# Dilated attention in a four-layer trunk: TensorE's weighted sums move between the two shares of the projection

## The chip, the cores and the metric

The kernel runs on one core of one Trainium2 chip. The metric is the device time of one execution in microseconds. Before the change it is 2908.95 us, the median of three runs (2908.55 to 2910.62).

## The reference

One sequence of 512 tokens, width 1024, four layers. Every layer is a token mixer and a squared-ReLU MLP, each behind an RMS norm and added to the residual. The mixers by layer are: dilated attention, indexer-selected sparse attention, gated DeltaNet, dilated attention. Only the two dilated ones (layers 0 and 3) are touched.

```python
qkv = (h @ w_in).reshape(B, S, 3, A_N_GROUPS, A_HEADS, HEAD_DIM)
q = rms_norm(qkv[:, :, 0], q_gain)          # per head
k = rms_norm(qkv[:, :, 1], k_gain)
for g, (window, dilation) in enumerate(((128, 1), (512, 4), (2048, 16))):
    o, lse = dilated_window_attention(q[:, :, g], k[:, :, g], v[:, :, g], bias_g, window, dilation)
wts = softmax(stack(lses), axis=0)          # mixture of the three dilations
y = sum(wts[..., None] * stack(outs), axis=0)
return y.reshape(B, S, A_OUT) @ w_out
```

## The kernel before

All matrix products with weights run as three products of rounded parts (high x high, high x low, low x high). ACT rounds a weight chunk to its high part (`rounding`, L695), GpSimd subtracts to get the low part (`split`, L555), TensorE multiplies. Every engine has its own list of instructions in program order, and semaphores tie the lists together; the order is written out by hand.

A dilated mixer works on heads in pairs: 4 pairs of 8 units, 32 units in all. Units 0 to 3 of a pair are the near group's four token blocks (one or two key blocks each), units 4 to 7 the two far groups, by residue class. A unit goes through this pipeline, and step s of a loop over 36 steps holds one stage of several units:

- TensorE `scores(s)` (L1856, L1863): queries times keys into banks 2 and 3. It waits until both halves of the logits of unit s-1 are out of these banks (`al_done`).
- DVE `logits(s)` (L1225): adds the bias and keeps the row's extreme value.
- ACT `probs(s)` (L868): exponential with a row sum, two halves.
- DVE `inverses(s-1)` (L1234): reciprocal of the sums, one step later.
- GpSimd `weights_scaled(s-1)` (L578): scales the probabilities by them.
- TensorE `turn(s-2)` (L1877): transposes them into bank 4 or 5.
- DVE (L1308), for the last pair ACT (L907): copies the transposes to SBUF.
- TensorE `weigh(s-3)` (L1893): weighted sum of the values, into bank 6. It waits for that copy.
- DVE `outputs(s-3)` (L1244): takes the sum out of bank 6.

Between these, TensorE computes the query and key projections of the next pairs: 18 tiles of 24 large matmuls (L1674), cut by `a_share` into 52 shares, two per step: `fill(2s)` and `fill(2s+1)`. So the shares end with step 25. A finished tile goes ACT square (L800) and copy with gain (L801), on DVE an epsilon term (L1208), then `sum_qk` on TensorE (L1801), which is issued at the end of the share after the one in which the tile ended; then ACT logarithm and exponential (L818, L820) and GpSimd `qk_scale` (L567). A tile's second half of a chunk also starts `rounding` and `split` of the chunk after next.

From step 26 on `joined` (L1719) puts parts of the output projection into the steps. At step 8f+1 `difference` (L1907) spreads the log sums of a finished pair, which DVE clamps (L1257), ACT turns into mixing weights at step 8f+2 (L897, L899, L901), and DVE mixes at step 8f+3 (L1263, L1266, L1268). ACT rounds the result (L911) and DVE takes its low part (L1272).

In a step, ACT's order is: `probs(s)`, the mixing operations if any, `part(2s)` (mean squares of a tile ended in share 2s-1, then square and copy of a tile ended in share 2s), the copy of unit s-2 for the last pair, `part(2s+1)`. DVE's order is: `inverses(s-1)`, `outputs(s-3)`, `logits(s)`, log sums, `part(2s)` (epsilon terms), mixing, the copy of unit s-2, `part(2s+1)`. GpSimd's is: `weights_scaled(s-1)`, second half of a split, the query or key scalings, first half of a split.

TensorE's two rules around the shares are:

```python
# fill(G): matmuls lo..hi of the tiles, then
for k, n, t in a_ended(i, G - 1):
    sum_qk(0, a_q(i, k, n, t))
# a_share(G): total = 24 * 6 * 3 = 432, A_FILL = 52
return min(total, total * G // A_FILL), min(total, total * (G + 1) // A_FILL)
```

Of the kernel before, what the change touches and what calls it, by code (L numbers as in the profile page):

```python
# [45 lines left out]
A_UNITS = A_PAIR_UNITS * A_PAIRS  # L46
# [51 lines left out]
def trunk(nc, x_in, rel_bias, params, c_gates, masks, bucket_rows, bias_mask, mlp_w1, mlp_w2,  # L98
# [20 lines left out]
    with ExitStack() as ctx:  # L119
# [287 lines left out]
        def a_blocks(u):  # L407

            return 1 if u % A_PAIR_UNITS == 0 else 2

        def a_near(u):
            return u % A_PAIR_UNITS < NB
# [6 lines left out]
        def a_share(G):  # L419

            total = 24 * 6 * (A_PAIRS - 1)
            return min(total, total * G // A_FILL), min(total, total * (G + 1) // A_FILL)

        def a_tiles(i):

            return [(k, chunk_at["aqk", i, k], tile0[chunk_at["aqk", i, k]] + j)
                    for k in range(3, 3 * A_PAIRS) for j in range(2)]

        def a_ended(i, G):

            lo, hi = a_share(G)
            return [x for j, x in enumerate(a_tiles(i)) if lo < 24 * j + 24 <= hi] if G >= 0 else []

        def a_q(i, k, n, t):

            return q_first[i] + 2 * k + t - tile0[n]
# [1202 lines left out]
        def _(pe):  # L1639
# [63 lines left out]
            def joined(i, j, pairs, lo, hi):  # L1703

                n0 = chunk_at["ao", i, 0]
                last = pairs[-1] == A_PAIRS - 1
                t = tile0[n0 + last] + j
                if lo == 0:
                    pe.wait_ge(w_lo_done, n0 + 1)
                    pe.wait_ge(*evac[t - 2])  # L1710
                for k in range(lo, hi):
                    f, z = pairs[k // 3], k % 3
                    if f >= 2 and z == 0:
                        pe.wait_ge(w_lo_done, n0 + 2)
                    w, a = ((w_hi, g_hi), (w_hi, g_lo), (w_lo, g_hi))[z]
                    c = DM * (f % 2) + P * j
                    if z == 0:
                        pe.wait_ge(yl_done, y_first[i] + f + 1)
                    mm = nc.tensor.matmul(lin_bank[t % 2][:], w[(n0 + f // 2) % 2][:].rearrange("p k n -> p (k n)")[:, c:c + P],  # L1719
                                          a[:, f, :], start=k == 0, stop=k == 3 * len(pairs) - 1)  # L1720
                if hi == 3 * len(pairs):
                    mm.then_inc(lin_done, 1)
# [69 lines left out]
            def sum_qk(kind, Q):  # L1792

                pe.wait_ge(qsq_done, Q + 1)
                if Q:
                    pe.wait_ge(qln_done, Q)
                if spread[0]:
                    pe.wait_ge(aclamp_done, spread[0])
                summed[0] = Q + 1
                sqs = mem[kind]["sq"]  # L1800
                nc.tensor.matmul(stat_bank[:], halves, sqs[Q % len(sqs)], start=True, stop=True).then_inc(ssq_done, 1)  # L1801

            def mixer_a(li, i):
                U0, F0, Q, Y = first_a[i], first_pair[i], q_first[i], y_first[i]

                def tile(n, t, lo, hi, act_sem=None):
                    product(n, t, H, CT, lo, hi, act_sem, 16 * li, None)
# [23 lines left out]
                def fill(G):  # L1831

                    lo, hi = a_share(G)
                    for j, (k, n, t) in enumerate(a_tiles(i)):
                        a, b = max(lo, 24 * j), min(hi, 24 * j + 24)
                        if a < b:
                            tile(n, t, a - 24 * j, b - 24 * j)
                    for k, n, t in a_ended(i, G - 1):
                        sum_qk(0, a_q(i, k, n, t))

                def scores(u):

                    f, z = divmod(u, A_PAIR_UNITS)
                    if z == 0:
                        pe.wait_ge(qk_ready, Q + 6 * f + 2)
                    if z == NB:
                        pe.wait_ge(qk_ready, Q + 6 * f + 6)
                    if u == 0:
                        pe.wait_ge(copied, copy_first[i] + 12)
                    if U0 + u:  # L1850
                        pe.wait_ge(al_done, 2 * (U0 + u))
                    if a_near(u):
                        n, k0 = P * a_blocks(u), P * max(z - 1, 0)
                        for half in range(2):
                            r = slice(HD * half, HD * half + HD)
                            mm = nc.tensor.matmul(bank[2 + half][:, 0:n], aq[f % 2][0][r, P * z:P * z + P],  # L1856
                                                  aq[f % 2][1][r, k0:k0 + n], start=True, stop=True)
                    else:
                        cols = slice(P * (z - NB), P * (z - NB) + P)
                        for g in (1, 2):  # L1860
                            for half in range(2):
                                r = slice(HD * half, HD * half + HD)
                                mm = nc.tensor.matmul(bank[2 + half][:, P * (g - 1):P * g],  # L1863
                                                      aq[f % 2][2 * g][r, cols], aq[f % 2][2 * g + 1][r, cols],
                                                      start=True, stop=True)
                    mm.then_inc(as_done, 1)

                def turn(u):

                    pe.wait_ge(an_done, 2 * (U0 + u + 1))  # L1870
                    if U0 + u >= 2:
                        pe.wait_ge(at_copied, U0 + u - 1)
                    nb = a_blocks(u)
                    for half in range(2):
                        for k in range(nb):
                            c = P * (nb * half + k)
                            mm = nc.tensor.transpose(bank[4 + u % 2][:, c:c + P], al[u % 4][:, half, P * k:P * k + P],  # L1877
                                                     ident)
                    mm.then_inc(at_turned, 1)

                def weigh(u):

                    f, z = divmod(u, A_PAIR_UNITS)
                    nb = a_blocks(u)
                    pe.wait_ge(at_copied, U0 + u + 1)
                    if U0 + u:
                        pe.wait_ge(ao_done, U0 + u)
                    for k in range(nb):
                        b, g = (z + 1 - nb + k, 0) if a_near(u) else (z - NB, 1 + k)
                        for half in range(2):  # L1890
                            c = (g * A_HEADS + 2 * f + half) * HD
                            p = P * (nb * half + k)
                            mm = nc.tensor.matmul(bank[6][HD * half:HD * half + HD, 0:P], av[:, b, c:c + HD],  # L1893
                                                  apt[u % 3][:, p:p + P], start=k == 0, stop=k == nb - 1)
                    mm.then_inc(apv_done, 1)

                def difference(f):

                    pe.wait_ge(alse_done, F0 + f + 1)
                    pe.wait_ge(qln_done, summed[0])  # L1900
                    lse = a_stat(f, 4)
                    for z in range(A_PAIR_UNITS):
                        for half in range(2):
                            rows = stat_bank[HD * half:HD * half + HD, :]
                            out = rows[:, P * z:P * z + P] if z < NB else by_class(rows)[:, z - NB, :]
                            c = 2 * z + half
                            mm = nc.tensor.matmul(out, lse[:, c:c + 1].to_broadcast([P, HD]), ident[:, ::-1], start=z == 0,  # L1907
                                                  stop=z == A_PAIR_UNITS - 1)
                    mm.then_inc(adelta_done, 1)
                    spread[0] = F0 + f + 1  # L1910
# [12 lines left out]
                    values(g)  # L1923
                for s in range(A_UNITS + 4):
                    f, z = divmod(s, A_PAIR_UNITS)
                    if 3 <= s < A_UNITS + 3:
                        weigh(s - 3)
                    if s < A_UNITS:
                        scores(s)
                    if 2 <= s < A_UNITS + 2:  # L1930
                        turn(s - 2)
                    fill(2 * s)
                    fill(2 * s + 1)
                    for j, lo, hi in A_EARLY.get(s, ()):
                        joined(i, j, (0, 1, 2), lo, hi)
                    if z == 1 and f:
                        difference(f - 1)
# [355 lines left out]
```

## Time and profile before

The profiled execution took 2909.07 us; its span is 2906.9 us.

| | busy, us | share of the span |
|---|---|---|
| TensorE, matmuls | 2800.9 | 96% |
| TensorE, weight loads | 2186.1 | 75% |
| DVE | 1015.0 | 35% |
| ACT | 1099.1 | 38% |
| GpSimd | 1378.0 | 47% |
| mean granted TensorE clock | 0.986 of full | |
| steps 0 to 25 of the first dilated mixer | from 146.5 to 314.8 us | |
| steps 26 to 35 of it | from 314.8 to about 356 us | |

How to read it: busy times overlap, so they say which engine has no room, and not what a change is worth. That is read from the engine that ends last in a stretch: its idle time, with what ended it, and the start times of its instructions. The durations of matmuls are modelled; the distance from one start to the next is what an instruction costs.

### The profile page before, as it was taken

The numbers are of one execution on the slowest core, as the hardware profiler recorded it, in microseconds if no ns is written. First come the engines' busy times: TensorE is split into PE (matmuls) and PEld (weight loads), VectorE is DVE, ScalarE is ACT, GpSimd is POOL, SyncE is SP. The second block draws the span as 40 slices with busy tenths as digits, with TensorE's granted clock in tenths as the row PEclk, the third lists the DMA queues.
The fourth block names the chain that finished last, engine by engine and source line by source line (L and its number), as shares of the span: only waits on it lengthen the run. The fifth ranks groups of instructions, "written<-read, shape, count | busy, mean of one in ns | idle before, by whom it ended". The sixth has DMA issues, their size and how long they took to land.

```text
span 2906.9 us, 39078 instructions
## 1 busy us (share of the span) xinstructions
PE 2800.9 (96%) x15534; PEld 2186.1 (75%) x15534; DVE 1015.0 (35%) x1906; ACT 1099.1 (38%) x1644; POOL 1378.0 (47%) x1073
## 2 busy tenths in 40 slices
PE   7999899999989999998899999999999999899999
PEld 5976678888756788887566666788887976688887
DVE  3034422113575512225466564311223044522112
ACT  4255433224445423333333433422334355532221
POOL 3467544445454445444243242345445467544443
PEclk8999999999989999999999999999999999999999
DMA  4331122323431232324111110232323331132332
GB/s 121 100 74 52 44 94 95 101 87 101 94 72 39 73 97 92 101 91 105 30 44 45 30 44 31 73 101 88 101 95 88 100 73 54 43 100 87 101 100 73
DMA packets 271762, 227.92 MB, mean 78 GB/s; under 512 B 30100, under 2 KB 259220, under 8 KB 271620
## 3 DMA queue, kind: packets, MB, share of 16 engines
q1 hardware_dynamic: 260880, 216.29, 24.7%
q10 hardware_dynamic: 10740, 9.65, 1.4%
q8 instruction: 100, 1.64, 0.2%
q14 instruction: 42, 0.34, 0.0%
HBM read 223.61 MB, written 2.30 MB: 78 GB/s over the span
## 4 chain that ended last, share of the span: by engine, by line
PE 88%; DVE 6%; ACT 3%; POOL 2%; issue 1%; DMA 0%; ACTq 0%; DVEq 0%; POOLq 0%
PE bank L1765 48%; PE bank L1674 18%; PE bank L2050 6%; PE bank L1826 5%; PE bank L1801 2%; PE bank L1719 1%; PE bank L1877 1%; POOL w_lo L555 1%; PE bank L1893 1%; PE bank L1979 1%; PE bank L2007 1%; PE bank L1992 1%; POOL arena L578 1%; PE bank L1863 1%; PE bank L1907 1%
## 5 line engine op out<-in xcount | busy, mean ns | idle before, releaser
L555 POOL TENSOR_TENSOR w_lo<-raw,w_hi 128x512 fp32r<-128x512 f32 x808 | 1070.0, 1355 | 1246.6 <-ACT w_hi L695 1246.6
L695 ACT ACTIVATE w_hi<-raw 128x2048 fp32r<-128x2048 f32 x202 | 385.5, 1908 | 465.3 <-PE bank L1765 423.3
L1765 PE MATMUL bank<-h_hi,w_hi 128*128 128x512 f32 x1024 | 400.8, 391 | 0.0
L1765 PE MATMUL bank<-h_hi,w_lo 128*128 128x512 f32 x1024 | 398.4, 389 | 0.0
L1765 PE MATMUL bank<-h_lo,w_hi 128*128 128x512 f32 x1024 | 398.4, 389 | 0.0
L1765 PE MATMUL bank<-g_hi,w_hi 128*128 128x512 f32 x1024 | 398.3, 389 | 0.0
L1765 PE MATMUL bank<-g_lo,w_hi 128*128 128x512 f32 x1024 | 398.3, 389 | 0.0
L1765 PE MATMUL bank<-g_hi,w_lo 128*128 128x512 f32 x1024 | 398.3, 389 | 0.0
L1674 PE MATMUL bank<-h_hi,w_hi 128*128 128x512 f32 x784 | 330.1, 421 | 6.9 <-POOL w_lo L555 4.6
L1674 PE MATMUL bank<-h_lo,w_hi 128*128 128x512 f32 x784 | 320.9, 409 | 0.0
L1674 PE MATMUL bank<-h_hi,w_lo 128*128 128x512 f32 x784 | 317.9, 405 | 0.0
L748 ACT ACTIVATE arena<-arena 128x512 f32<-128x512 f32 x128 | 80.9, 632 | 425.9 <-DVE arena L1175 425.9
L1765 PEld LDWEIGHTS bank<-h_hi,w_hi 128*128 128x128 f32 x1024 | 192.2, 188 | 41.2 <-issue 1.4
L1765 PEld LDWEIGHTS bank<-h_lo,w_hi 128*128 128x128 f32 x1024 | 192.3, 188 | 41.0 <-issue 1.4
L1765 PEld LDWEIGHTS bank<-g_hi,w_lo 128*128 128x128 f32 x1024 | 192.2, 188 | 39.9
L1765 PEld LDWEIGHTS bank<-h_hi,w_lo 128*128 128x128 f32 x1024 | 192.2, 188 | 39.9
L1765 PEld LDWEIGHTS bank<-g_hi,w_hi 128*128 128x128 f32 x1024 | 192.2, 188 | 39.9
L1765 PEld LDWEIGHTS bank<-g_lo,w_hi 128*128 128x128 f32 x1024 | 192.2, 188 | 39.8
L1175 DVE SCALAR_TENSOR_TENSOR arena<-bank,rs 128x512 f32<-128x512 f32 x128 | 88.5, 692 | 373.0 <-PE bank L1765 349.5
L1190 DVE TENSOR_TENSOR x<-x,bank 128x512 f32<-128x512 f32 x96 | 66.0, 687 | 431.6 <-PE bank L1765 431.6
L2050 PEld LDWEIGHTS bank<-arena 128*64 128x64 f32 x3172 | 144.5, 138 | 74.5 <-issue 33.8
L2050 PE MATMUL bank<-arena 128*64 128x64 f32 (+2 forms) x3172 | 192.6, 265 | 4.8 <-DVE arena L1526 3.2
(233 smaller groups left out, 3764.3 us busy)
## 6 DMA issues: line engine op xcount, KB each, us to landing
raw<-in_mlp_w SPq DMA_DIRECT2D x128, 1024.0 KB, 5.4
raw<-in_a_w_in SPq DMA_DIRECT2D x48, 512.0 KB, 5.1
raw<-in_c_w_in SPq DMA_DIRECT2D x32, 512.0 KB, 5.5
raw<-in_a_w_in SPq DMA_DIRECT2D x12, 1024.0 KB, 5.1
raw<-in_b_w_in SPq DMA_DIRECT2D x18, 256.0 KB, 4.2
raw<-in_a_w_out SPq DMA_DIRECT2D x4, 1024.0 KB, 4.8
raw<-in_b_w_in SPq DMA_DIRECT2D x4, 1024.0 KB, 5.3
arena<-bias_scratch ACTq DMA_DIRECT2D x16, 256.0 KB, 3.6
```

The costliest lines, as they stand in the source:

```text
L555: ins = nc.gpsimd.tensor_tensor(w_lo[s][:, k, :], raw[s][:, k, :], w_hi[s][:, k, :].bitcast(F32), ALU.subtract)
L578: nc.gpsimd.tensor_scalar(t, t, a_stat(u // A_PAIR_UNITS, 2)[:, c:c + 1], None, ALU.mult).then_inc(an_done, 1)
L695: nc.scalar.activation(w_hi[s][:], raw[s][:], ACT.Copy).then_inc(w_hi_done, 1)
L748: nc.scalar.activation(gsq[j % 2], relu_t[j % 2], ACT.Square).then_inc(gsq_done, 1)
L1175: nc.vector.scalar_tensor_tensor(relu_t[j % 2], lin_bank[j % 2][:], 0.0, rs, ALU.max, ALU.mult).then_inc(relu_done, 1)
L1190: nc.vector.tensor_tensor(x[:, c, :], x[:, c, :], lin_bank[c % 2][:], ALU.add).then_inc(x_added, 1)
L1674: mm = nc.tensor.matmul(o, lhsT, rhs, start=start, stop=stop)
L1719: mm = nc.tensor.matmul(lin_bank[t % 2][:], w[(n0 + f // 2) % 2][:].rearrange("p k n -> p (k n)")[:, c:c + P], a[:, f, :], start=k == 0, s ...
L1765: mm = nc.tensor.matmul(lin_bank[j][:], w[s][:, c, P * j:P * j + P], a[:, c, :], start=c + z == 0, stop=c == CT - 1 and z == 2)
L1801: nc.tensor.matmul(stat_bank[:], halves, sqs[Q % len(sqs)], start=True, stop=True).then_inc(ssq_done, 1)
L1826: mm = nc.tensor.matmul(bank[2 + b][:], keys, quads[w][:, c, :], start=half + c + z == 0, stop=half == 1 and c == 3 and z == 2)
L2050: mm = nc.tensor.matmul(out[z:z + HD], lhsT[:, z:z + HD], rhs, start=start, stop=stop)
```

## The change

In a step of the dilated mixers' loop on TensorE, the weighted sums of unit s-3 are issued behind the scores of unit s, the transposes of unit s-2 and the first share of the projection, and ahead of the second share. The lists of the other engines are not touched, and no wait or count is changed.

```diff
                 for s in range(A_UNITS + 4):
                     f, z = divmod(s, A_PAIR_UNITS)
-                    if 3 <= s < A_UNITS + 3:
-                        weigh(s - 3)
                     if s < A_UNITS:
                         scores(s)
                     if 2 <= s < A_UNITS + 2:
                         turn(s - 2)
                     fill(2 * s)
+                    if 3 <= s < A_UNITS + 3:
+                        weigh(s - 3)
                     fill(2 * s + 1)
                     for j, lo, hi in A_EARLY.get(s, ()):
                         joined(i, j, (0, 1, 2), lo, hi)
```

## Rows read from the trace of the kernel before

**Rows 1.** TensorE's waits, first dilated mixer (144 to 360 us): total us, times, longest us.

```profile
PE bank L1893 <- ACT arena L907: 4.7, 3, 2.7
PE bank L1877 <- POOL arena L578: 3.9, 3, 1.4
PE bank L1719 <- DVE g_lo L1272: 2.3, 1, 2.3
PE bank L1801 <- DVE sq L1208: 0.9, 1, 0.9
PE bank L1907 <- ACT sq L818: 0.8, 1, 0.8
```

**Rows 2.** Timeline of TensorE, start of step 14, then of step 34: start, duration, instruction.

```profile
232.18 0.39 PE L1674 MATMUL bank<-h_hi,w_hi 128*128 128x512 f32 x1
232.50 0.66 PE L1893 MATMUL bank<-arena 128*64 128x128 f32 x8
233.08 0.71 PE L1863 MATMUL bank<-arena 64*128 64x128 f32 x8
233.73 0.66 PE L1877 MATMUL bank<-com,arena 128*128 128x128 f32 x4
234.14 0.48 PE L1674 MATMUL bank<-h_lo,w_hi 128*128 128x512 f32 x1
...
349.71 0.50 PE L1719 MATMUL bank<-g_hi,w_hi 128*128 128x512 f32 x1
350.05 0.39 PE L1719 MATMUL bank<-g_lo,w_hi 128*128 128x512 f32 x1
350.28 0.40 PE L1719 MATMUL bank<-g_hi,w_lo 128*128 128x512 f32 x1
```

**Rows 3.** Timeline of DVE in steps 14 and 16.

```profile
233.20 0.29 DVE L1244 COPY arena<-bank 128x128 f32<-128x128 f32 x1 [0.90 <-PE bank L1893]
...
246.20 0.37 DVE L1244 COPY arena<-bank 128x128 f32<-128x128 f32 x1
246.40 0.28 DVE L1225 CUSTOM_DVE_ANT_0 arena<-bank,arena 128x128 f32<-128x128 f32 x1
```

**Rows 4.** Timeline of all engines in step 10; then DVE's group, 147 to 314 us.

```profile
207.95 0.42 DVE L1225 CUSTOM_DVE_ANT_0 arena<-bank,arena 128x256 f32<-128x256 f32 x1
...
208.42 0.51 ACT L868 ACTIVATE arena<-arena 128x256 f32<-128x256 f32 x1 [4.37 <-DVE arena L1225]
...
209.42 0.62 ACT L897 ACTIVATE rs<-ss 128x512 f32<-128x512 f32 x1
...
211.37 0.58 ACT L800 ACTIVATE sq<-bank 128x512 f32<-128x512 f32 x1
...
211.98 0.69 DVE L1208 TENSOR_TENSOR sq<-sq,em 128x512 f32<-128x512 f32 x1 [3.25 <-ACT sq L800]
...
212.72 1.12 PE L1801 MATMUL bank<-sq,com 128*128 128x512 f32 x2 [0.89 <-DVE sq L1208]
...
L1208 DVE TENSOR_TENSOR sq<-sq,em 128x512 f32<-128x512 f32 x18 | 19.5, 1084 | 39.2 <-ACT sq L800 39.2
```

**Rows 5.** Timeline of ACT and TensorE, steps 14 to 16; last, the second dilated layer.

```profile
237.34 1.91 ACT L695 ACTIVATE w_hi<-raw 128x2048 fp32r<-128x2048 f32 x1
...
238.12 1.06 PE L1801 MATMUL bank<-sq,com 128*128 128x512 f32 x2
...
247.06 0.66 PE L1877 MATMUL bank<-com,arena 128*128 128x128 f32 x4 [1.38 <-POOL arena L578]
...
2425.32 0.66 PE L1877 MATMUL bank<-com,arena 128*128 128x128 f32 x4 [1.37 <-POOL arena L578]
```

**Rows 6.** ACT's copy of unit 24; stretches: us, PE busy, PEclk, DMA share, GB/s.

```profile
320.77 0.58 ACT L907 ACTIVATE arena<-bank 128x512 f32<-128x512 f32 x1
...
321.40:325.90 4.50, 4.50 (x18) 0.62 0.33 75
2534.60:2538.00 3.40, 2.88 (x10) 1.00 0.00 0
```

## The prediction

> **What bounds the kernel now.** I read the table of engines first: TensorE is busy for 2800.9 of 2906.9 us, every other engine for less than half. So a change counts only where TensorE stands still, is fed differently, or has its clock lowered. Next, TensorE's waits inside one dilated mixer [rows 1]: 12.6 us in these rows, of 216. By place they are two kinds. In steps 0 to 25, where the remaining projections fill the gaps, TensorE is nearly without a pause (one wait for VectorE's epsilon sum, three for GpSimd's scaling, one for ScalarE ahead of `difference`). In steps 26 to 35, without projection work, there are three waits of the weighted sums for ScalarE's copy (4.7 us) and one at the end. The second dilated layer repeats this to a hundredth [rows 5]. Last I followed single steps in the timelines [rows 2 to 6]; what they show is slack on ACT and DVE that the present order gives them.
>
> **The change, part by part.** No instruction is added or dropped. In a step s, `weigh(s-3)` (8 records on TensorE) goes behind `scores(s)`, `turn(s-2)` and the first share `fill(2s)`.
>
> *(a) One more switch between large and small matmuls per step.* Two large ones start 0.23 us apart; from the last large one to `weigh` it takes 232.50 - 232.18 = 0.32, from `weigh` to the next large one's successor 0.34 (350.05 - 349.71) where 0.23 is normal [rows 2]. Before, a step has big, weigh, scores, turn, big; after, big, scores, turn, big, weigh, big. Extra: 0.09 + 0.11 = 0.20 us. It is paid where both shares hold work, steps 3 to 25, so 23 x 2 layers x 0.20 = 9.2 us. Steps 26 to 35 have no fills and pay nothing. Bounds: 0 (if only the modelled ends move) to 0.25 each, so 0 to 11.5; I take the rows' own value. The Trainium skill (TensorE: Matmul & The Clock Gate, section "Step-by-step: what each phase is for") says that TensorE pulls the next weight load ahead of running matmuls; by that the switch would be free and this term 0. The rows disagree, 0.32 against 0.23, and I go by them.
>
> *(b) DVE and ACT get their work later, and a projection tile waits behind it.* DVE's order in a step is fixed: `outputs(s-3)`, which waits for `weigh(s-3)`, then `logits(s)`. ACT's is `probs(s)`, which waits for `logits(s)`, then the evacuation of any tile that ended in this step's first share. So the late `weigh` holds logits, probabilities, the square of that tile (L800), its epsilon sum on DVE (L1208) and then TensorE itself, which asks for it in `sum_qk` at the end of `fill(2s+1)`. Call W the start of `weigh`. Chain: W to `outputs` 0.70 (233.20 - 232.50); to `logits` 0.20 (246.40 - 246.20, scores long done); to `probs` 0.47; `probs` 1.00 until ACT is free; square to epsilon sum 0.61; epsilon sum to `sum_qk` 0.74 [rows 2, 3, 4]. Sum 3.72 us. TensorE has only 0.59 (`weigh`, 233.08 - 232.50) + 0.11 + 8 or 9 x 0.23 = 2.54 or 2.77 us of work between [rows 2]. Before, it had scores 0.65, transposes 0.41 and a whole share more, 3 us, which was the cover. Stall: 1.18 with eight matmuls, 0.95 with nine.
>
> Which steps? `a_share` gives 432/52 = 8.31 matmuls per share, and a tile of 24 ends in an even share for G = 8, 14, 20, 28, 34, 40, 46, that is steps 4, 7, 10, 14, 17, 20, 23 (G = 2 has no `weigh` yet). Nine matmuls follow in steps 4, 14, 17, eight in 7, 20, 23. Step 10 is special: ACT has three more operations between `probs` and the square (209.42 to 211.37, 1.95 us), TensorE already waits 0.89 there [rows 4], and afterwards it would wait 1.18 + 1.95 = 3.13, that is 2.24 more. Per layer 3 x 0.95 + 3 x 1.18 + 2.24 = 8.6, both layers 17.3 us. Tiles that end in an odd share have scores, transposes and a share behind them as before, and cost nothing here.
>
> The 0.74 belongs to an epsilon sum of 0.69 us; the 18 of a layer average 1.08, being slower beside GpSimd [rows 4]. 14 of them x 0.39 = 5.5 us at most, 0 at least; I take half, 2.7, because the late sum meets GpSimd in other places.
>
> *(c) GpSimd's chain.* The transposes of unit 14 wait 1.38 for a chain that begins with the `sum_qk` at 238.12: root mean square on ACT, query scaling, a weight split, the units' scaling [rows 5]. It ends at a fixed 247.06 - 238.12 = 8.94 us behind `sum_qk`, whatever TensorE does meanwhile. Three such waits per layer [rows 1]. In the new order `weigh` (0.59 + 0.20) no longer lies ahead of the transposes but behind, so it is added once the wait is over; the 0.40 of (a) in the two steps is swallowed by the wait. The tile's rounding on ACT (from 237.34, 1.91 us long) now finishes after `sum_qk` rather than with it, about +0.3. So 0.7 x 6 = 4.2 us; bounds 0 and 1.3 x 6 = 7.8.
>
> *(d) Two small ones.* In step 11 the three mixing operations stand on DVE between logits and the next tile's epsilon sum: about 0.3 late; and `difference` in step 17 waits for the same ACT work as in (c), 0.4. Both layers: 1.4 us, an estimate, 0 to 4.
>
> *(e) The clock.* A 3.1 us pause is as long as the longest seen. After the pause of 2.7 us that ends at 321.40 [rows 1] the granted clock was 0.62 for 4.5 us; behind 2534.6, where the other layer's wait for L1272 (2.3 in the first) ends, it stayed at 1.00 [rows 6]. At a mean of 0.62, that is for the most part at 1.2 instead of 2.4 GHz, 4.5 us hold 4.5 x 0.38 = 1.7 us less work. I charge this once per layer for step 10: 3.4 us (0 to 3.4; if the pauses of 1 us lowered it too, more).
>
> *(f) Steps 26 to 35.* Here `weigh` waits for copies on ACT, and scores and transposes now go first. That hides 1.1 us of each wait. But the copy at 320.77 starts when ACT comes free of its own queue, not when the transposes end [rows 6], and that queue begins with `probs(26)`, which is later by scores, transposes and a `sum_qk` (0.65 + 0.3 + 0.95 = 1.9, of which 0.5 is regained as the DVE no longer waits for scores). So the copy comes about 1.4 later, and what is gained is a broken pause that may keep the clock up: -0.4 per layer, -0.8 us (bounds -12.8, all three waits and the clock's loss, and +3).
>
> Loads do not enter: no transfer is among the releasers of TensorE's waits in this part [rows 1], and the slots' order stays.
>
> **Sum.** 9.2 + 17.3 + 2.7 + 4.2 + 1.4 + 3.4 - 0.8 = +37.4 us. The profiled execution took 2909.07 us, its span 2906.9, and the median of the three is 2908.95; the difference is nothing. Forecast 2946 us, 1.3% slower.
>
> **Rivals.** *Only the switch is paid.* If the square, the epsilon sum and `sum_qk` were early enough (the chain of 3.72 measured too long, or the evacuation not really behind `probs`), 9.2 - 0.8 would remain: 2917 us. For it: TensorE waited for a square only once in a layer so far [rows 1]. Against: both engines run their lists in order, and the chain in step 10 is seen link by link [rows 4]. *Nothing at all:* with the skill's free switch too, 2909 us, within 0.2%.
>
> *Faster.* One mechanism: in steps 27, 29 and 30 the sums stop waiting for ACT's copy, 4.7 us, and the low clock behind the first, 1.7; twice that is 12.8, so 2896 us if steps 3 to 25 cost nothing. It decides as soon as the copy's start is set by the transposes. Against it: ACT's own queue sets it, in (f), and (a) and (b) would have to be nearly zero together.
>
> *It feeds on itself.* If scores had to wait for the previous logits as well: these end at W + 0.70 + 0.20 + 2 x 0.42 = 1.74, scores come at W + 2.5 [rows 2 to 4]. Slack 0.8 us, so not in a plain step; if it did by 0.5 in half of the steps, +12 more: 2958 us.
>
> **How the numbers follow.** Forecast case (a to f near their values) 0.68; only the switch 0.12; self-feeding 0.08; nothing 0.07; faster 0.05. The terms' bounds make the forecast's own range 2928 to 2955 (switch at half, no clock and no GpSimd term at the low end; contention and small terms in full at the high end). The range from 2922 to 2957 reaches toward both neighbours. About 0.2% (5.8 us) is what a measurement can tell from no change: faster 0.05, same 0.07, slower 0.88; the switch alone, 2917, still counts as slower.
>
> **What would show each step.** TensorE's waits at L1801 for DVE's L1208: seven per layer of about 1 us, the one in step 10 about 3; if they are missing, (b) is wrong and with it half of the sum. `logits` (L1225) should follow `outputs` (L1244) by 0.2 with no wait for scores. Waits for GpSimd at L1877 in steps 16, 22 and 25 of 1 to 2 us. A granted clock under 1.00 after step 10. Waits for L907 about as before. Large to `weigh` and back at 0.32 and 0.34 apart. The rest of the kernel unchanged: a difference outside the two dilated mixers would be beyond this argument.

## The result and the profile after

The changed kernel takes 2951.14 us, median of four runs (2950.42 to 2952.66), against 2909.43 us of the kernel before measured beside it: a ratio of 1.0145, 95% interval 1.013 to 1.0159, so 41.7 us slower. The forecast was 2946, range 2922 to 2957. One execution of the run below that moves step 10 alone took 4914.6 us at a mean granted clock of 0.715; it is left out of that run's figures.

TensorE's waits of the changed kernel in the first dilated mixer (144 to 400 us: total us, times, longest):

```profile
PE bank L1801 <- DVE sq L1208: 10.4, 7, 3.0
PE bank L1877 <- POOL arena L578: 3.4, 4, 1.6
PE bank L1719 <- DVE g_lo L1272: 3.0, 2, 2.3
PE bank L1893 <- ACT arena L907: 2.3, 1, 2.3
...
PE bank L1907 <- ACT sq L818: 1.2, 3, 0.8
PE bank L1863 <- DVE arena L1225: 1.1, 1, 1.1
PE bank L1801 <- DVE ss L1257: 0.6, 1, 0.6
```

Beside [rows 1]: `sum_qk` (L1801) waited once for the epsilon sum, 0.9 us, and now waits seven times, 10.4 us. The copies on ACT (L907) cost 4.7 us and now 2.3. The granted clock of the same layer, by stretches (us; PE busy; PEclk; DMA share; GB/s):

```profile
145.75:219.20 73.45, 67.70 (x378) 1.00 0.31 72
219.20:226.40 7.20, 7.15 (x19) 0.58 0.00 0
226.40:272.80 46.40, 42.42 (x235) 1.00 0.23 57
272.80:277.20 4.40, 4.32 (x38) 0.61 0.00 0
277.20:334.40 57.20, 52.34 (x309) 1.00 0.17 56
```

Two stretches of steps 3 to 25 run at a low clock, the first behind step 10's wait of 3.0 us; the kernel before had none there. What they cost is 7.2 x 0.42 + 4.4 x 0.39 = 4.7 us in this layer, and as much in the other.

The books of one layer, from scores of unit 0 to the start of step 26: before 314.82 - 146.53 = 168.3 us, after 334.46 - 145.75 = 188.7 us, 20.4 more. Waits 14.7 against 5.8, +8.9; clock +4.7; 23 switches of 0.20, +4.6; and 6 x 0.28 = 1.7 for starting again after a wait, which the idle time does not hold (below; six, since the kernel before has one of the seven). That makes 19.9; 0.5 is not placed. Steps 26 to 35 take 1.6 more. Both layers alike, so 44; the stretches outside give 2 back, almost all of it between the two layers (1966.2 against 1968.4 us), with nothing changed in them.

The chain that the forecast put into numbers, as it runs in step 7 of the changed kernel; first TensorE, then DVE, then ACT (start, duration):

```profile
190.50 0.39 PE L1674 MATMUL bank<-h_hi,w_hi 128*128 128x512 f32 x1
190.82 0.66 PE L1893 MATMUL bank<-arena 128*64 128x128 f32 x8
191.41 0.50 PE L1674 MATMUL bank<-h_lo,w_hi 128*128 128x512 f32 x1
191.75 0.40 PE L1674 MATMUL bank<-h_hi,w_lo 128*128 128x512 f32 x1
...
193.15 0.40 PE L1674 MATMUL bank<-h_hi,w_lo 128*128 128x512 f32 x1
194.97 1.13 PE L1801 MATMUL bank<-sq,com 128*128 128x512 f32 x2 [1.43 <-DVE sq L1208]
```

```profile
191.53 0.40 DVE L1244 COPY arena<-bank 128x128 f32<-128x128 f32 x1 [3.75 <-PE bank L1893]
191.75 0.42 DVE L1225 CUSTOM_DVE_ANT_0 arena<-bank,arena 128x256 f32<-128x256 f32 x1
...
193.83 1.09 DVE L1208 TENSOR_TENSOR sq<-sq,em 128x512 f32<-128x512 f32 x1 [1.29 <-ACT sq L800]
```

```profile
192.22 0.51 ACT L868 ACTIVATE arena<-arena 128x256 f32<-128x256 f32 x1 [3.50 <-DVE arena L1225]
...
193.23 0.57 ACT L800 ACTIVATE sq<-bank 128x512 f32<-128x512 f32 x1
```

From `weigh` at 190.82: outputs +0.71, logits +0.22, probabilities +0.47, square +1.01, epsilon sum +0.60, `sum_qk` +1.14. DVE sat idle 3.75 us before the outputs, waiting for `weigh`. TensorE's last large matmul starts at 193.15, and it stands until 194.97. A large matmul normally lets the next start after 0.23 us; here its whole 0.40 passes before idle time is counted, so a wait costs its idle time and 0.17 more; and from this `sum_qk` to the next scores it takes 1.06, where 0.95 is what it takes when `sum_qk` did not wait. That is the 0.28 above.

### The profile page after: what moved, and what is told of

It is laid out like the page before. It is cut to its first block, busy times and chain, and to the rows that moved or that the text cites. A ratio compares the mean times of both kernels' runs of the same rounds, so it can differ in the third digit from the quotient of the medians.

```text
span 2948.7 us, 39078 instructions
## 1 busy us (share of the span) xinstructions
PE 2827.4 (96%) x15534; PEld 2188.5 (74%) x15534; DVE 1005.4 (34%) x1906; ACT 1095.1 (37%) x1644; POOL 1370.7 (46%) x1073
## 4 chain that ended last, share of the span: by engine, by line
PE 87%; DVE 6%; ACT 4%; POOL 2%; issue 1%; DMA 0%; ACTq 0%; DVEq 0%; POOLq 0%
PE bank L1765 47%; PE bank L1674 18%; PE bank L2050 6%; PE bank L1826 5%; PE bank L1801 2%; PE bank L1719 1%; PE bank L1893 1%; PE bank L1877 1%; POOL w_lo L555 1%; PE bank L1979 1%; ACT arena L868 1%; PE bank L2007 1%; ACT w_hi L695 1%; PE bank L1992 1%; PE bank L1863 1%
```

## The experiments

All times are medians beside the kernel before on the same chip (2907.6 to 2908.4 us there); differences are against that.

### Which steps lose: shares, tail, seven steps, sixteen steps

One condition decides where the weighted sums stand, with `late` being `s < 26`, `s >= 26`, `s in (4, 7, 10, 14, 17, 20, 23)`, or the other sixteen:

```diff
+                    late = s in (4, 7, 10, 14, 17, 20, 23)
-                    if 3 <= s < A_UNITS + 3:
+                    if 3 <= s < A_UNITS + 3 and not late:
                         weigh(s - 3)
...
                     fill(2 * s)
+                    if 3 <= s < A_UNITS + 3 and late:
+                        weigh(s - 3)
                     fill(2 * s + 1)
```

> The weighted sums move behind the first share only in steps 0 to 25, where there are shares; steps 26 to 35 keep the old order. Theory (the loss lies in the late logits, the seven projection tiles behind them, the switch and the clock, all in steps 3 to 25; in the changed kernel these steps take 20.4 us more per layer): 2 x 20.4 = +41 us, about 2950. Rival (the tail of the mixer loses too): clearly less than the changed kernel's +42, by 3 us or more. Rival (the tail gains and hides a larger loss): above +42.

Measured: 2948.81, +40.4 us, ratio 1.0148 (1.0131 to 1.0165). The loss is in steps 3 to 25. TensorE's lists and waits there are those of the changed kernel (14.7 us of waits per layer in both), yet steps 0 to 25 take 185.6 us in this trace's first layer and 188.5 in its second, against 188.7 in both layers of the changed kernel. The clock makes the difference. Behind step 17's two waits, 1.20 and 0.78 us in either layer, it was (first layer, then second):

```profile
270.80:276.40 5.60, 4.80 (x44) 1.00 0.00 0
2469.80:2474.20 4.40, 4.33 (x38) 0.61 0.01 4
```

And behind step 10's 3.0 us it was low for 4.0 us in the first layer and for 6.2 in the second. So up to 3 us per layer of the loss comes or stays away with the same instructions and the same waits.

> The weighted sums move only in steps 26 to 35. Forecast's step (f): -0.8 us, since the copies on ACT set the pace. Rival (three waits for the copy and the low clock behind the first go away): -12.8 us, 2896. From the changed kernel's trace, where these steps take 43.3 us against 41.6: +3 us.

Measured: 2908.35, -0.1 us, ratio 1.000 (0.9991 to 1.001). The tail neither gains nor loses. The rival that gave 2896 is out. Why the waits for L907 shrink and nothing is won, the trace of this run shows (TensorE's waits, 320 to 384 us):

```profile
PE bank L1719 <- DVE g_lo L1272: 3.0, 2, 2.3
PE bank L1893 <- ACT arena L907: 1.8, 1, 1.8
PE bank L1863 <- DVE arena L1225: 1.1, 1, 1.1
PE bank L1877 <- POOL arena L578: 0.8, 1, 0.8
```

The 4.7 us for the copies became 1.8, and waits for logits (1.1), GpSimd (0.8) and a low part (0.7 beyond the 2.3 that stays) came in: 4.4.

> The weighted sums move only in steps 4, 7, 10, 14, 17, 20 and 23, where a projection tile ends in the first share. Theory: per layer 10.4 - 0.9 us of waits for the epsilon sum, 4.7 us for two stretches at low clock, 7 x 0.2 for the switch and about 0.8 for restarts, 2 x 16.4 = +33 us. Rival (each late step costs about the same): 7 of 23 steps, +12.5 us.

Measured: 2942.50, +34.1 us, ratio 1.0115 (1.0098 to 1.0132). In its trace the epsilon sum is waited for 7 times, 10.4 us, as in the changed kernel. Seven steps of 23 carry five sixths of the loss; that each step costs alike is refuted, and with it that only the switch is paid.

> The weighted sums move in the other sixteen of steps 3 to 25 and stay in those seven. Theory: only the switch between large and small matmuls is paid, 2 x 16 x 0.20 = +6.4 us, with no wait for the epsilon sum and no low clock; up to 3 us more if GpSimd's chain grows. Rival (each late step costs about the same): 16 of 23, +28 us.

Measured: 2920.50, +12.1 us, ratio 1.0043 (1.0026 to 1.006). More than the switch, and its trace says what (TensorE's waits, 144 to 320 us):

```profile
PE bank L1877 <- POOL arena L578: 3.1, 3, 1.6
PE bank L1893 <- DVE arena L1308: 2.3, 2, 1.8
...
PE bank L1907 <- ACT sq L818: 1.2, 3, 0.8
PE bank L1801 <- DVE sq L1208: 0.9, 1, 0.9
```

The one wait for an epsilon sum is the old one. New are two waits of `weigh` for DVE's copy, in steps 17 and 20, where a late step is followed by an early one and the copy has no room. Steps 0 to 25 take 5.2 us more per layer, 1.6 of it waits (7.4 against 5.8), and 3.6 / 16 = 0.22 us per switch is left, near the rows' 0.20.

### One step, and the clock

The same edit with `late = s == 10`.

> The weighted sums move in step 10 alone, where ACT has three mixing operations ahead of the tile's square. Theory: per layer the wait grows from 0.9 to 3.0 us (+2.1), the switch costs 0.2, and the clock is low for 7.2 us behind it at a mean of 0.58 (3.0 us lost, as in the changed kernel's stretch at 219 us): 5.3 x 2 = +10.6 us. The forecast's own price of the clock (1.7 us): +8.1. Rival (no clock change from a single pause of 3 us): +4.6.

Measured: 2917.51, +9.9 us, ratio 1.0032 (1.0018 to 1.0046). In the trace steps 0 to 25 take 172.1 us against 168.3 in either layer, so 3.8 more: 2.1 of wait (3.0 against the 0.9 that was there), 0.2 for the switch, and 4.3 us at a granted clock of 0.60, which is 1.7 lost. The price of the clock here is the forecast's 1.7, not the 3.0 that was expected from the changed kernel's stretch of 7.2 us. The rest came in the first layer's steps 26 to 35, where nothing was moved: 44.1 us against 41.6, behind the same wait of 2.73 us for the copy. The clock there:

```profile
324.40:332.00 7.60, 7.20 (x35) 0.55 0.43 138
334.20:338.60 4.40, 4.39 (x25) 0.61 0.00 0
```

In the kernel before it was 0.62 for 4.5 us [rows 6], and this kernel's second layer takes 41.6 there as before. So the expected +10.6 was met by luck: a low clock in another place made up for the shorter one in step 10.

For the next one the changed kernel's ACT list is turned round in step 8f+2:

```diff
+                    part(2 * s)
                     if z == 2 and f:
                         act.wait_ge(aclamp_done, F0 + f)
...
-                    part(2 * s)
```

> The changed kernel, with ACT's three mixing operations of step 8f+2 issued behind the work on the projection tile instead of ahead of it. Theory: the wait in step 10 falls from 3.0 to about 1.2 us like the other six, and the low clock behind it goes: per layer 1.8 + 3.0 us, +42 - 9.6 = +32 us against the kernel before. Rival (the clock falls anyway at seven waits of a microsecond): +42 - 3.6 = +38.

Measured: 2939.05, +31.5 us, ratio 1.0109 (1.0092 to 1.0126). The trace has the wait in step 10 at 1.02 us. It also has step 17, which is where the changed kernel's second slow stretch began. First the changed kernel, then this one:

```profile
270.97 1.13 PE L1801 MATMUL bank<-sq,com 128*128 128x512 f32 x2 [1.21 <-DVE sq L1208]
272.88 3.52 PE L1907 MATMUL bank<-com,arena 128*64 128x128 f32 x32 [0.78 <-ACT sq L818]
```

```profile
268.34 1.13 PE L1801 MATMUL bank<-sq,com 128*128 128x512 f32 x2 [1.21 <-DVE sq L1208]
270.24 1.97 PE L1907 MATMUL bank<-com,arena 128*64 128x128 f32 x32 [0.78 <-ACT sq L818]
```

The same two waits, 1.21 and 0.78 us with one `sum_qk` between, were followed in the one kernel by a stretch at 0.61 (`difference` 3.52 us long) and in the other by 1.00 (1.97 us). So this second stretch is not set by the length of the waits alone, as the two layers of the run with steps 0 to 25 moved also show. What decides, these runs do not settle. The expected +32 was met although it left this second stretch in.

### Is it DVE's order?

The changed kernel with two calls on DVE exchanged; TensorE's list stays as it is.

```diff
-                    if 3 <= s < A_UNITS + 3:
-                        outputs(s - 3)
                     if s < A_UNITS:
                         logits(s)
+                    if 3 <= s < A_UNITS + 3:
+                        outputs(s - 3)
```

> The changed kernel, with DVE's outputs(s-3) issued behind logits(s) instead of ahead of it; nothing is left out. Theory (the late weighted sum holds the logits only through DVE's order): the seven waits for the epsilon sum go, with them both stretches of low clock, and only the switch is left, +9.2 us against the kernel before, up to +14 with GpSimd's chain. Rival (the projection tile waits for something else, ACT's own load or the sum_qk behind the matmuls): stays near +42.

Measured: 2922.59, +15.0 us, ratio 1.0049 (1.0033 to 1.0066). No wait for the epsilon sum is left; steps 0 to 25 show only these (144 to 320 us):

```profile
PE bank L1877 <- POOL arena L578: 4.0, 3, 1.7
...
PE bank L1907 <- ACT sq L818: 0.8, 1, 0.8
```

So two lines on DVE take back 27 of the 42 us: the late weighted sum did its harm through the outputs that stand ahead of the logits. The rest is 6.0 us per layer in steps 0 to 25 (4.6 of switches and 1.8 of one slower stretch, at 0.91 from 280 to 300 us, less 1.0 of waits, is 5.4; 0.6 is not placed) and 1.4 in the tail, where the clock is at 0.52 for 7.1 us.

### What a switch costs, and the waits for GpSimd

In the kernel before, the transposes go between the shares, in all of steps 2 to 25 or only in 16, 22 and 25:

```diff
-                    if 2 <= s < A_UNITS + 2:
+                    if 2 <= s < A_UNITS + 2 and not behind:
                         turn(s - 2)
                     fill(2 * s)
+                    if 2 <= s < A_UNITS + 2 and behind:
+                        turn(s - 2)
                     fill(2 * s + 1)
```

> The kernel before, with the transposes between the two shares in all steps 2 to 25: one more switch between large and small matmuls in each of 24 steps, and nothing on the other engines is held by it, since the copy that follows has a whole step. Theory (a switch costs 0.20 us): 24 x 2 x 0.20 = +9.6, less the 3.9 us per layer of waits for GpSimd that the first share covers, +1.8 us. Rival (the switch is free, as the skill's rule on weight loads would have it; Trainium skill, TensorE: Matmul & The Clock Gate, section Step-by-step): -7.8 us.

Measured: 2905.64, -2.8 us, ratio 0.9992 (0.9982 to 1.0001), between the two and not clearly told from no change. All waits for GpSimd are gone. The expectation's 0.20 was wrong for this switch (timeline of TensorE, step 5 of this kernel):

```profile
178.36 0.40 PE L1674 MATMUL bank<-h_hi,w_hi 128*128 128x512 f32 x1
178.59 0.60 PE L1877 MATMUL bank<-com,arena 128*128 128x128 f32 x4
178.95 0.48 PE L1674 MATMUL bank<-h_lo,w_hi 128*128 128x512 f32 x1
179.27 0.39 PE L1674 MATMUL bank<-h_hi,w_lo 128*128 128x512 f32 x1
```

From a large matmul to a transpose of full height and width it takes the usual 0.23, where `weigh` (128 x 64) and scores (64 x 128) take 0.32. The way back has the 0.32 there too. Steps 0 to 25 in this trace are 165.45 us against 168.3, with 4.2 less of waits, so 24 of these switches cost 1.4 us, 0.06 each. Both layers gain that 2.8; 1.4 us are lost in the second layer's steps 26 to 35, where the clock is low for longer, with the waits as before.

> The kernel before (weighted sums first), but in steps 16, 22 and 25 the transposes stand between the two shares, so that the first share covers their wait for GpSimd. Theory: 3.9 us of waits per layer go and three switches of 0.2 us come, -6.6 us, 2902. Rival (GpSimd is itself late there, and the wait comes back at the next step's transposes or as a wait for the copy): within 2 us of the kernel before.

Measured: 2900.86, -6.7 us, ratio 0.9978 (0.9968 to 0.9987). In steps 0 to 25 TensorE waits for GpSimd no more, and they take 4.0 us less per layer. This kernel is faster than the kernel before and the changed one. The expectation came out at -6.6 with 0.20 for a switch; with the 0.06 just found the same sum is -7.4.

### The mixing operations and the tail's copy in the kernel before

First the exchange on ACT of the run above, made in the kernel before.

> The kernel before, with ACT's three mixing operations behind the work on the projection tile. Theory: the one wait of 0.9 us in step 10 goes, -1.8 us in all; nothing else follows, since the mixing on DVE comes a step later. Rival (the mixing comes late for the tail): +1 to +4.

Measured: 2905.55, -2.9 us, ratio 0.9991 (0.9981 to 1.000), at the edge of what can be told from no change; the wait in step 10 is gone. Next, the copy of the last pair moves up on ACT:

```diff
                         probs(s)
+                    if 2 <= s < A_UNITS + 2 and s - 2 >= 3 * A_PAIR_UNITS:
+                        u = s - 2
+                        act.wait_ge(at_turned, U0 + u + 1)
+                        act.wait_ge(apv_done, U0 + u - 2)
+                        nc.scalar.activation(apt[u % 3], bank[4 + u % 2][:], ACT.Copy).then_inc(at_copied, 1)
                     if z == 0 and f:
                         logs(f - 1)
...
                     part(2 * s)
-                    if 2 <= s < A_UNITS + 2 and s - 2 >= 3 * A_PAIR_UNITS:
...
                     part(2 * s + 1)
```

> The kernel before, with ACT's copy of the transposes (last pair) issued right behind the probabilities instead of behind mixing and mean squares. Forecast's step (f) says that ACT's own queue sets this copy: the wait of 2.7 us and the low clock behind it go, a wait of about 1 us for GpSimd's scaling takes their place, 1.9 + 1.6 us per layer, -7 us; at least -3. Rival (the transposes set the copy): no change within 1 us.

Measured: 2911.66, +3.2 us, ratio 1.0013 (1.0003 to 1.0022). The half about ACT's queue holds: the copy starts at 317.22, right behind the probabilities, where it was at 320.77 behind mixing and mean squares [rows 6]. The gain does not come (TensorE's waits, 314 to 357 us; L897 is the moved copy in this kernel):

```profile
PE bank L1877 <- POOL arena L578: 2.4, 2, 1.5
PE bank L1863 <- POOL arena L567: 1.7, 1, 1.7
PE bank L1893 <- ACT arena L897: 0.9, 2, 0.7
```

GpSimd's scaling of the last keys (L567) stands behind a weight split and starts when it did before, at 322.94; TensorE arrives earlier and waits for that, 1.7 us, then for the units' scaling. 4.7 us of waits became 5.0 (4.5 in the second layer), which alone would be nearly no change. The loss goes with the clock, low for longer in both layers than the 4.5 us at 0.62 of [rows 6]:

```profile
327.00:335.00 8.00, 7.31 (x40) 0.57 0.10 37
2501.50:2513.00 11.50, 9.10 (x50) 0.55 0.30 93
```

> The kernel before with three edits: transposes between the shares in steps 16, 22 and 25, ACT's mixing operations behind the projection tile, ACT's copy of the last pair right behind the probabilities. If their gains add up: -6.7 - 1.8 - 7 = -15.5 us, 2893. Rival (the waits of the tail take each other's place): -8 to -10.

Measured: 2902.24, -6.2 us, ratio 0.998 (0.9971 to 0.999). This is the kernel before with the three moved transposes, the exchange on ACT and the copy moved up, all at once: no better than the transposes alone. The three measured one by one add up to the same, -6.7 - 2.9 + 3.2 = -6.4, so the tail's edit takes back what the exchange would add.

## Why the prediction was right

The direction and the main mechanism, (a) and (b), are shown. That the number came as near as 5 us is partly luck: two other terms missed by 6 us each, in opposite directions.

**What bounds the kernel** held: the late work on DVE and ACT shows where TensorE's list meets it. The stretches outside the dilated mixers gave back 2 us, with none of their instructions touched; the forecast had called such a difference beyond its argument.

**(a) The switch.** 0.32 into the weighted sums and 0.34 behind them, in the rows after as in [rows 2]; 0.22 by the sixteen steps. The Trainium skill's rule that the next weight load is pulled ahead of running matmuls when the row groups do not conflict or it goes to the background weight buffer (TensorE: Matmul & The Clock Gate, section "Step-by-step: what each phase is for"), read as the forecast read it, would have made it free. For `weigh` the 0.32 says it is not; for the way into full-size transposes the row shows nothing to pay.

**(b) The chain through DVE and ACT.** The mechanism is shown, link by link, and by the exchange on DVE. The seven steps are the seven named, and their waits are 1.02 to 1.43 us and 3.0 (forecast 0.95 to 1.18 and 3.13). The term was 17.3 + 2.7 = 20 us for both layers. Measured it is 2 x (9.5 + 1.7) = 22.4: the last link is 1.14 in step 7, not 0.74, since the epsilon sum runs 1.09 us there, and the cost of starting again was missing in the sum. The forecast put the longer sums down to GpSimd working beside them. That is not what the trace shows here: GpSimd's last work ends at 193.58, before this sum starts at 193.83. What makes it 1.09 and not 0.69 is open. The rival that feeds on itself is out: in steps 0 to 25 no scores wait for logits.

**(c) GpSimd's chain.** Mis-sized, and with the wrong sign. Its waits in steps 16, 22 and 25 are 0.87, 1.58 and 0.64, in sum 3.1 against 3.9 before, where 1 to 2 us each was forecast. The distance that was called fixed, 8.94 us from `sum_qk` to the transposes, is 257.59 - 249.44 = 8.15 in the changed kernel. The link that is shorter is the units' scaling on GpSimd; first the kernel before, with DVE's epsilon sum of the next tile beside it, then the changed kernel, where that sum starts later (256.85):

```profile
244.34 2.67 POOL L578 TENSOR_SCALAR arena<-arena 128x256 f32<-128x256 f32 x2
245.12 1.09 DVE L1208 TENSOR_TENSOR sq<-sq,em 128x512 f32<-128x512 f32 x1 [2.81 <-ACT sq L800]
...
255.70 1.83 POOL L578 TENSOR_SCALAR arena<-arena 128x256 f32<-128x256 f32 x2
```

That the epsilon sum is what lengthened the scaling is not tested. Forecast +4.2 for both layers; the waits fell by 1.7.

**(d)** `difference` waits 1.2 instead of 0.8 us in all, but not as said: its wait in step 17 stayed at 0.78, and 0.2 came in at steps 9 and 25. No wait came from the mixing in step 11.

**(e) The clock** was, with (c), the term furthest off: 3.4 us said, 9.4 in the trace. Behind the 3.0 us wait the low clock lasted 7.2 us, not 4.5, and a second stretch came in step 17, where two pauses of 1.2 and 0.8 us lie close together. The forecast had named this only as "if the pauses of 1 us lowered it too". What failed is that one stretch, read once, was taken as the price of a pause. The kernel before spoke against it: behind its wait of 2.3 us for L1272 the clock stayed at 1.00 in the second layer [rows 6], and in the first it was

```profile
356.40:360.20 3.80, 3.77 (x10) 0.55 0.00 0
```

The run with steps 0 to 25 moved puts up to 3 us per layer on this. That this one profiled execution holds the larger amount in both layers is chance, as far as the runs tell.

**(f) The tail.** Forecast -0.8, alone -0.1 us. The reason holds that ACT's own queue sets the copy: it comes 8.2 us behind the start of step 26 (342.68 - 334.46) where it was 6.0, so 2.3 later and not 1.4. The sign "waits for L907 about as before" failed: they fell from 4.7 to 2.3 us, and others took their place. With steps 3 to 25 changed as well, the tail takes 1.6 us more per layer in the trace, and the runs put it at 1.3 us for both (41.7 less 40.4), which is less than the clock alone moved between the two layers of one run.

So the sum of +37.4 was 4 us short: (b) 2.5, (e) 6 and (f) 2 to 4 too little, (c) and (d) about 6.5 too much, 1 not placed, and 2 us came back outside the mixers.

## What to carry to other kernels

Before a group is moved down an engine's list, look at what the consumer's engine does right behind its wait for it: here the taking of a weighted sum stood ahead of logits that were ready, and everything that a third engine does for the next product stood behind those. Count the work that is left between the moved group and the next thing asked of the chain, by step, for steps with different contents lose differently. A wait on the busiest engine that has no such cover can be moved behind one share of independent work, if nothing on the other engines is held by it: three moved transposes won 6.7 us. And do not charge a low clock by the length of the pause in front of it: here the same pause was followed by different clocks, so that a difference of 2 to 3 us can be the clock's.

## What the runs showed of the hardware

- The switch from 128x512 matmuls costs 0.09 us into 128 x 64 or 64 x 128 forms, none into 128 x 128 transposes, and 0.09 to 0.11 on the way back. A whole extra switch came to 0.22 us for the weighted sums (sixteen steps) and to 0.06 for the transposes (24 steps).
- A wait of TensorE costs its idle time and about 0.28 us more where a 0.23 us stream of large matmuls is broken: 0.17 that the modelled end hides, and 0.11 at the restart.
- Behind the pause of 3.0 us in step 10 the granted clock was low in both layers of all four kernels that had it, but for 7.2 us in the changed one (at 0.58) and for 4.3 us in the one with step 10 alone moved (at 0.60). The same pair of pauses, 1.2 and 0.78 us, was followed by 0.61 in one kernel and 1.00 in another, and by both in the two layers of one execution.
- DVE's epsilon sum (128x512, f32) took 0.69 or 1.09 us with no GpSimd instruction beside it, and up to 1.76 us with one in the kernel before's first dilated mixer.
